# A fp32 decoder block on one core: reordered start, a shorter inverse root, and last stores from two queues

## The chip, the cores and the metric

The kernel runs on one core of one Trainium2 chip. The metric is device time in microseconds (us), the median of several runs. The profile is one execution of its own.

## The reference

The reference computes one decoder block on x of shape (1, 256, 2048) in float32:

```
x = x + 0.5 * swiglu(rms_norm(x, g1), wg1, wu1, wd1)     # 2048 -> 5632 -> 2048
h = rms_norm(x, gm)
b, c, xv, q, k, v = split(h @ w_in)                       # six parts of 1024 columns
y_conv = b * causal_depthwise_conv(c * xv, conv_w)        # 3 taps
a = softmax(q1 k1) - lam * softmax(q2 k2), causal         # 8 differential heads
y_attn = rms_norm(a @ v, subln_w) * (1 - lambda_init)
x = x + concat(y_conv, y_attn) @ w_out
x = x + 0.5 * swiglu(rms_norm(x, g2), wg2, wu2, wd2)
out = rms_norm(x, final_norm)
swiglu(x, wg, wu, wd) = (silu(x @ wg) * (x @ wu)) @ wd
```

## The kernel before

Every large product is a stream of weight chunks. A chunk is a [128, 2, 512] tile of float32 (512 KB: two blocks of 128 rows by 512 columns of a weight matrix). There are 656 of them, and each passes a ring of four slots (`RING = 4`) on its way: SyncE (SP) loads it into `raw[slot]` (`load`, L236 to L241), ScalarE (ACT) makes its high part `w_hi = fp32r(raw)` (`high`, L484 to L489), VectorE (DVE) makes its low part `w_lo = raw - w_hi` (`low`, L656 to L660), and TensorE (PE) multiplies (`unit`, L285 to L302). The activations are split in the same way into `xT_hi` and `xT_lo`. For each of two row tiles and two blocks of the chunk TensorE does three matmuls (hi by hi, hi by lo, lo by hi), so a chunk is 12 matmuls of 128x512.

Each engine runs a list of instructions written out by hand, in program order, and the engines meet at counting semaphores. The order around the change is therefore just the order of the statements:

- **Start.** SP loads a quarter of x (512 KB) and a chunk in turns, four times (L251 to L253), then goes on with chunks; a chunk from the fifth on waits for `lo_ready` of the one that had its slot. ACT first issues the loads of the column constants (`cols`, L571) and of the lambda rows (L572). TensorE turns the first two quarters of x (`turn_x`, L326 to L333, eight 128x128 transposes each, written to PSUM), does the first chunk, turns the third quarter, does the second chunk, turns the last quarter. ACT does `high(g)` and then `split_x` of quarter g, for g = 0 to 3 (L576 to L578); DVE does `low(g)` and the same split (L787 to L789). POOL (GpSimd) makes the identity matrix (L897 to L900) and then loads the final norm's weights, 1 MB when spread over 128 rows (`gfin`, L919). TensorE waits for chunk k's part of xT by `turned_lo`.
- **Inverse root.** `inverse_root` (L689 to L697) computes 1/sqrt of a mean of squares on VectorE: the mean (L691), a first guess from the bits in two steps (L692, L693), and three Newton steps of three instructions each (L695 to L697). Each one waits for the one in front of it (`link`, L98 to L101). It is used at the end of each of the first three norms' sums (`norm_factor`, both row tiles at once), once per head in the mixer (L828, eight heads), and for each row tile at the very end (`finish`, L712 to L723).
- **Mixer.** Two passes `j`, each of 48 chunks; the four heads' attention steps are laid between the chunks by their number `s`. The last step of a head: `inverse_root`, then `head = bank * orstd` (L830), then a transpose on TensorE (`turn_head`, L426 to L431). At a pass's end VectorE does the convolution (L866 to L874), ACT splits it (L638), and then both go back to the chunks.
- **End.** In the last pair of columns the last four chunks are done for row tile 0 first and then for row tile 1. For each tile VectorE adds the residual (L763), ACT squares it (L519), POOL multiplies by `gfin` (L932), `finish(t)` makes the factor, ACT scales the even groups of 512 columns (`scale_last`, L511), VectorE the odd ones (L723), and SP stores the four pieces of 256 KB in the order 0, 1, 2, 3 (L275 to L279).

Of the kernel before, what the change touches and what calls it, by code (L numbers as in the profile page):

```python
# [27 lines left out]
F32 = mybir.dt.float32  # L28
# [5 lines left out]
P = 128  # L34
# [25 lines left out]
MAGIC = float(0x5F3759DF)  # L60
NEWTON = 3

# [29 lines left out]
class Steps:  # L92
# [9 lines left out]

    def enter(self, i, each):

        self.outer, self.each, self.base, self.n = self.base + self.n, each, self.base + self.n + i * each, 0
# [6 lines left out]
def hybrid_block(nc, x_in, wg1, wu1, wd1, w_in, w_out, wg2, wu2, wd2, gf, columns, lambdas, out):  # L112
    ctx = ExitStack()
    with ctx:
# [16 lines left out]
        spare = sb("spare", [P, 1])  # L131
        ident = sb("ident", [P, P])
# [53 lines left out]
        gfin_loaded = sem("gfin_loaded")  # L186
        hi_ready = sem("hi_ready")
# [47 lines left out]
        def _(sp):  # L235
# [11 lines left out]
            def gate_up(base, wg, wu, c, first=False):  # L247
                for u, w in enumerate((wg, wu)):
                    for k in range(CD):
                        n = base + 2 * CD * c + CD * u + k  # L250
                        if first and u == 0 and k < XG:  # L251
                            load_x(k)
                        load(n, k % RING, w, k, c * W)  # L253
# [8 lines left out]
            gate_up(CH_FFN1, wg1, wu1, 0, first=True)  # L262
# [12 lines left out]
            for t in range(TT):  # L275
                for g in range(XG):
# [7 lines left out]
        def _(pe):  # L284
# [18 lines left out]

            def banks_free(pair, second):
# [21 lines left out]
            def turn_x(g):  # L326
                if g == 0:
                    pe.wait_ge(ident_ready, 2)
# [3 lines left out]
                for t in range(TT):  # L332
                    turn(x[:, :, g * W:(g + 1) * W], T_LOW if g % 2 == 0 else T_HIGH, t, turned)  # L333

            def gate_up(ch, pr, tbx, c, first=False, start=False):
                for second in range(2):
                    banks_free(pr + c, second)
                    for k in range(CD):
                        if first and second == 0:
                            pe.wait_ge(turned_lo, tbx + k + 1)  # L340
                        unit(ch + 2 * CD * c + CD * second, second, xT_hi, xT_lo, CD, k)
                        if start and second == 0 and k + 2 < XG:
                            turn_x(k + 2)
# [89 lines left out]

            turn_x(0)
            turn_x(1)
# [47 lines left out]
        def _(act):  # L483
# [7 lines left out]
            def split_x(tb, banks, gain, hi, k0):  # L491
                for b in range(2):
# [11 lines left out]

            def scale_last(t):
# [27 lines left out]
            def gate_up(ch, pr, hid, norm, c, first=False, start=False):  # L533
                base = ch + 2 * CD * c
                for n in range(2 * CD):
# [11 lines left out]
                    high(base + n + RING, n % RING)  # L547
                    if start and 2 <= n < 2 + XG:
# [22 lines left out]
            act.dma_start(cols[:], columns).then_inc(cols_loaded, 16)  # L571
            act.dma_start(lam_rows, lambdas.rearrange("(o a) d -> o a d", o=1).broadcast_to([P, 4, DK]))\  # L572
               .then_inc(lam_loaded, 16)

            act.wait_ge(cols_loaded, 16)
# [403 lines left out]
```

## Time and profile before

| | us |
|---|---|
| median of 3 runs | 1863.37 |
| lowest, highest | 1862.76, 1864.0 |
| span of the profiled execution, first to last instruction | 1861.2 |
| TensorE busy in it | 1835.5 |
| VectorE busy | 1128.0 |
| ScalarE busy | 834.9 |

The page gives the profiled execution's own time only as its span, 1861.2 us. The median of the runs is 2.2 us above that: what lies in front of the first and behind the last instruction, and what one execution differs from another. In the page the PE line is matmuls, PEld the weight loads beside them; a busy time is the union of instructions that overlap in the pipeline. Lines such as L295 are those of the kernel before.

### The profile page before, as it was taken

To read this page: it belongs to the slowest core of one execution; us is meant where nothing else is said; L and a number is where in the kernel's file an instruction comes from. 1 tells how busy PE (TensorE), PEld (TensorE's weight loads), DVE (VectorE), ACT (ScalarE), POOL (GpSimd) and SP (SyncE) were. 2 spreads that over 40 slices of the span, in tenths; PEclk is the share of its full clock that TensorE was granted. 3 is DMA by queue.
4 is the path that set the end of the run, shared out by engine and by line. 5 is a ranking of instruction groups with operands and counts; after the bars stand their busy time and mean duration, and the time that the engine had idled before them with its cause. 6 is when DMAs were issued, how large, how long until landed. Compare 5 with 4: busy or idle time off the path is not lost.

```text
span 1861.2 us, 24044 instructions
## 1 busy us (share of the span) xinstructions
PE 1835.5 (99%) x8184; PEld 1509.5 (81%) x8184; DVE 1128.0 (61%) x1519; ACT 834.9 (45%) x993; POOL 26.8 (1%) x36
## 2 busy tenths in 40 slices
PE   7999999999999999999999999999999999999997
PEld 6888888888888888888788788888888888888886
DVE  5666666666654554557547755666666666654554
ACT  6444444444444444455445444444444444443443
POOL 0000000000000000000000000000000000000000
PEclk9999999999999999999999999999999999999999
DMA  7666666666655556555564556666666666656653
GB/s 254 198 193 193 192 192 192 193 192 191 192 195 188 184 188 192 182 170 169 171 185 141 191 178 183 193 192 193 192 192 195 193 190 192 191 195 195 192 191 127
DMA packets 181155, 350.02 MB, mean 188 GB/s; under 512 B 10864, under 2 KB 10992, under 8 KB 180976
## 3 DMA queue, kind: packets, MB, share of 16 engines
q1 hardware_dynamic: 180672, 348.17, 61.0%
q0 software_dynamic: 144, 1.05, 0.1%
q8 instruction: 26, 0.43, 0.1%
q10 hardware_dynamic: 288, 0.17, 0.1%
q14 instruction: 25, 0.20, 0.0%
HBM read 347.25 MB, written 2.10 MB: 188 GB/s over the span
## 4 chain that ended last, share of the span: by engine, by line
PE 96%; DVE 1%; issue 1%; ACT 1%; DMA 1%; ACTq 0%; SPq 0%; DVEq 0%
PE bank L295 32%; PE bank L296 31%; PE bank L297 31%; PE bank L314 1%; DMA x<-in_x_dram 1%; PE bank L405 0%; ACT w_hi L489 0%; PE bank L422 0%; DVE turn_in L763 0%; PE bank L391 0%; DVE conv L871 0%; PE bank L413 0%; PE bank L430 0%; DVE nt L695 0%; DVE w_lo L659 0%
## 5 line engine op out<-in xcount | busy, mean ns | idle before, releaser
L659 DVE TENSOR_TENSOR w_lo<-raw,w_hi 128x1024 fp32r<-128x1024 f32 x656 | 808.7, 1235 | 694.3 <-ACT w_hi L489 692.4
L489 ACT ACTIVATE w_hi<-raw 128x1024 fp32r<-128x1024 f32 x656 | 693.3, 1059 | 875.8 <-PE bank L297 863.6
L295 PE MATMUL bank<-w_hi,xT_hi 128*128 128x512 f32 x1792 | 702.4, 392 | 1.6 <-DVE w_lo L659 1.5
L297 PE MATMUL bank<-w_hi,xT_lo 128*128 128x512 f32 x1792 | 698.4, 390 | 0.0
L296 PE MATMUL bank<-w_lo,xT_hi 128*128 128x512 f32 x1792 | 698.0, 390 | 0.0
L295 PEld LDWEIGHTS bank<-w_hi,xT_hi 128*128 128x128 f32 x1792 | 336.9, 188 | 73.8 <-issue 3.2
L297 PEld LDWEIGHTS bank<-w_hi,xT_lo 128*128 128x128 f32 x1792 | 336.8, 188 | 70.4
L296 PEld LDWEIGHTS bank<-w_lo,xT_hi 128*128 128x128 f32 x1792 | 337.1, 188 | 69.1
L295 PE MATMUL bank<-w_hi,hT_hi 128*128 128x512 f32 x704 | 276.7, 393 | 0.1
L296 PE MATMUL bank<-w_lo,hT_hi 128*128 128x512 f32 x704 | 275.8, 392 | 0.0
L297 PE MATMUL bank<-w_hi,hT_lo 128*128 128x512 f32 x704 | 274.2, 389 | 0.0
L679 DVE STREAM_TRANSPOSE gate<-turn_in 32x256 f32<-32x256 f32 x352 | 153.4, 436 | 5.7
L297 PEld LDWEIGHTS bank<-w_hi,hT_lo 128*128 128x128 f32 x704 | 132.1, 188 | 30.1
L295 PEld LDWEIGHTS bank<-w_hi,hT_hi 128*128 128x128 f32 x704 | 132.2, 188 | 29.4 <-issue 0.3
L296 PEld LDWEIGHTS bank<-w_lo,hT_hi 128*128 128x128 f32 x704 | 132.3, 188 | 27.3
L295 PE MATMUL bank<-w_hi,yT_hi 128*128 128x512 f32 x128 | 50.4, 393 | 0.0
L297 PE MATMUL bank<-w_hi,yT_lo 128*128 128x512 f32 x128 | 50.2, 392 | 0.0
L296 PE MATMUL bank<-w_lo,yT_hi 128*128 128x512 f32 x128 | 50.2, 392 | 0.0
L545 ACT ACTIVATE gate<-bank,rstd 128x512 f32<-128x512 f32 x44 | 30.1, 690 | 19.4 <-DVE hT_lo L686 10.5
L503 ACT ACTIVATE hT_hi<-gate 128x1024 f32 (+1 forms) x22 | 23.4, 1064 | 30.2 <-DVE gate L679 30.2
L740 DVE SCALAR_TENSOR_TENSOR turn_in<-bank,rstd,gate 128x512 f32<-128x512 f32 x44 | 30.9, 743 | 0.0
L295 PEld LDWEIGHTS bank<-w_hi,yT_hi 128*128 128x128 f32 x128 | 24.0, 188 | 5.6 <-issue 0.5
(95 smaller groups left out, 420.7 us busy)
## 6 DMA issues: line engine op xcount, KB each, us to landing
raw<-in_ffn_w_gate_dram SPq DMA_DIRECT2D x176, 512.0 KB, 3.8
raw<-in_ffn_w_up_dram SPq DMA_DIRECT2D x176, 512.0 KB, 3.7
raw<-in_ffn_w_down_dram SPq DMA_DIRECT2D x176, 512.0 KB, 3.8
raw<-in_w_in_dram SPq DMA_DIRECT2D x96, 512.0 KB, 3.7
raw<-in_w_out_dram SPq DMA_DIRECT2D x32, 512.0 KB, 3.8
x<-in_x_dram SPq DMA_DIRECT2D x4, 512.0 KB, 10.3
out_dram<-x SPq DMA_DIRECT2D x8, 256.0 KB, 3.2
gfin<-in_final_norm_dram POOLq DMA_DIRECT2D x1, 1024.0 KB, 9.6
```

Of the source, the lines that this page charges most:

```text
L295: pe.matmul(acc, hi[:, kt, ts], w_hi[slot][:, kk], start=(k == 0 and kk == 0), stop=False)
L296: pe.matmul(acc, hi[:, kt, ts], w_lo[slot][:, kk], start=False, stop=False)
L297: mm = pe.matmul(acc, lo[:, kt, ts], w_hi[slot][:, kk], start=False, stop=(k == chunks - 1 and kk == KC - 1))
L314: mm = pe.transpose(bank[banks[b]][:, kk * SEQ + t * P:kk * SEQ + (t + 1) * P], src[:, t, blk * P:(blk + 1) * P], ident[:])
L489: act.activation(w_hi[slot][:], raw[slot][:], ACT.Copy).then_inc(hi_ready, 1)
L503: act.activation(hT_hi[:, bass.ds(BT * c, BT), :], hidT, ACT.Copy).then_inc(hid_hi, 1)
L545: act.activation(gate[:, t], bank[t][:], ACT.Silu, scale=rstd[:, t:t + 1])\
L659: dve.tensor_tensor(w_lo[slot][:], raw[slot][:], w_hi[slot][:].bitcast(F32), ALU.subtract)\
L679: v = dve.transpose(dst[32 * j:32 * j + 32, :, :, i], src[32 * i:32 * i + 32, :, :, j])
L740: dve.scalar_tensor_tensor(out=turn_in[:, t], in0=bank[2 + t][:], scalar=rstd[:, t:t + 1], in1=gate[:, t], op0=ALU.mult, op1=ALU.mult).the ...
```

## The change

It has seven parts.

1. **Loads at the start** (SP). The first chunk comes in two halves of 256 KB (`first_chunk`), and the order is: quarter 0 of x, the two halves, chunk 1, quarter 1, chunks 2 and 3, quarters 2 and 3, then the other chunks. The lambda rows are loaded after ACT's fourth `high`, and `gfin` (POOL queue) after the first feed-forward's last save, some 740 us later.
2. **ScalarE at the start.** A one-element Silu in front of everything (`spare_out`), which loads the activation table; the later table load in front of the first real Silu is gone from the list. Then: half of the split of quarter 0, the first chunk's two halves, the other half of the split, chunk 1, the split of quarter 1, chunks 2 and 3. Quarters 2 and 3 are split between later chunks. VectorE follows the same order, and its small lambda work comes after the first norm factor.
3. **TensorE at the start.** 14 transposes of the identity into bank 7, which nobody reads, then quarter 0; then the first chunk in an order of its own (`first_unit`: hi by hi of both row tiles, lo of x by hi, hi by lo), quarter 1, chunk 1, quarter 2, chunks 2 and 3, quarter 3.
4. **Inverse root.** The guess is one instruction, each Newton step two, on `[P,1]` operands with one or two operands read as per-partition scalars. The results grow by a factor of 2^13, which is taken out by one more instruction in `norm_factor`, by a second multiplication in the head's scaling, and by `gfin` at the end. Where both row tiles are wanted (three norms, eight heads), each step is two instructions, one per tile, and each waits for the one before the last (`settle`).
5. **gfin scaled.** ACT multiplies `gfin` (128x2048) by 2^-13 behind the mixer's last pass.
6. **finish.** The sums of the first groups are divided by D and get EPS beforehand, so the mean is one instruction from `sq` and `ssum`.
7. **Last stores.** SP stores groups 1, 0, 3; ACT stores group 2 itself.

```diff
-MAGIC = float(0x5F3759DF)
+MAGIC = float(0x5F3759DF - 2 ** 31)
+GROWN = [3.0, 12.0, 768.0]
+SHRINK = 2.0 ** -13
+WARM = 14
...
@@ SyncE
+            def first_chunk(w):
+                src = w[0].rearrange("(k p) n -> p k n", p=P)
+                sp.dma_start(raw[0][:, 0], src[:, 0, 0:W]).then_inc(half_loaded, 16)
+                sp.dma_start(raw[0][:, 1], src[:, 1, 0:W]).then_inc(raw_loaded[0], 16)
...
-            gate_up(CH_FFN1, wg1, wu1, 0, first=True)
+            load_x(0)
+            first_chunk(wg1)
+            load(1, 1, wg1, 1, 0)
+            load_x(1)
+            load(2, 2, wg1, 2, 0)
+            load(3, 3, wg1, 3, 0)
+            load_x(2)
+            load_x(3)
+            gate_up(CH_FFN1, wg1, wu1, 0, opened=RING)
...
-                for g in range(XG):
+                for g in (1, 0, 3):
                     sp.wait_ge(scaled[g % 2], (t * XG + g) // 2 + 1)
@@ TensorE
+            def first_unit():
+                for kk in range(KC):
+                    pe.wait_ge(half_hi if kk == 0 else hi_ready, 1)
+                    if kk == 0:
+                        pe.wait_ge(turned_hi, TB_X1 + 1)
+                    for t in range(TT):
+                        pe.matmul(bank[t][:], xT_hi[:, kk, t * P:(t + 1) * P], w_hi[0][:, kk], start=(kk == 0), stop=False)
+                    if kk == 0:
+                        pe.wait_ge(turned_lo, TB_X1 + 1)
+                    for t in range(TT):
+                        pe.matmul(bank[t][:], xT_lo[:, kk, t * P:(t + 1) * P], w_hi[0][:, kk], start=False, stop=False)
+                    pe.wait_ge(half_lo if kk == 0 else lo_ready, 1)
+                    for t in range(TT):
+                        mm = pe.matmul(bank[t][:], xT_hi[:, kk, t * P:(t + 1) * P], w_lo[0][:, kk], start=False, stop=False)
+                mm.then_inc(chunk_used, 1)
...
+            pe.wait_ge(ident_ready, 2)
+            for _ in range(WARM):
+                pe.transpose(bank[7][:, 0:P], ident[:], ident[:])
             turn_x(0)
-            turn_x(1)
@@ ScalarE
+                act.wait_ge(scaled[0], (t + 1) * XG // 2)
+                act.dma_start(out[0, t * P:(t + 1) * P, cs], x[:, t, cs]).then_inc(stored, 16)
...
+            act.wait_ge(spare_ready, 1)
+            act.activation(spare_out[:], spare[:], ACT.Silu)
...
+            act.wait_ge(gfin_loaded, 16)
+            act.activation(gfin[:], gfin[:], ACT.Copy, scale=SHRINK).then_inc(gfin_scaled, 1)
@@ VectorE
-            def inverse_root(v_out, sums, y, width, t=slice(0, TT)):
-                link(dve.tensor_scalar(v_out, sums, 1.0 / width, EPS, ALU.mult, ALU.add))
-                link(dve.tensor_scalar(y.bitcast(I32), v_out.bitcast(I32), 1, None, ALU.logical_shift_right))
-                link(dve.tensor_scalar(y.bitcast(I32), y.bitcast(I32), -1.0, MAGIC, ALU.mult, ALU.add))
-                for _ in range(NEWTON):
-                    link(dve.tensor_tensor(nt[:, t], v_out, y, ALU.mult))
-                    link(dve.scalar_tensor_tensor(out=nt[:, t], in0=nt[:, t], scalar=-0.5, in1=y, op0=ALU.mult, op1=ALU.mult))
-                    link(dve.scalar_tensor_tensor(out=y, in0=nt[:, t], scalar=1.5, in1=y, op0=ALU.add, op1=ALU.mult))
+            def inverse_root(v, y, ts):
+                def each(make):
+                    for t in ts:
+                        steps.settle(len(ts) - 1)
+                        steps.mark(make(slice(t, t + 1)))
+                each(lambda t: dve.tensor_scalar(y[:, t].bitcast(I32), v[:, t].bitcast(I32), -0.5, MAGIC, ALU.mult, ALU.add))
+                for n in range(NEWTON):
+                    each(lambda t: dve.tensor_scalar(nt[:, t], y[:, t], y[:, t], v[:, t], ALU.mult, ALU.mult))
+                    each(lambda t: dve.tensor_scalar(y[:, t], nt[:, t], GROWN[n], y[:, t], ALU.subtract, ALU.mult))
+                steps.settle(0)
...
-                link(dve.tensor_tensor(ssum[:, ts], ssum[:, ts], sq[:, ts], ALU.add))
-                inverse_root(nv[:, ts], ssum[:, ts], rstd[:, ts], D, ts)
+                link(dve.tensor_scalar(nv[:, ts], sq[:, ts], 1.0 / D, ssum[:, ts], ALU.mult, ALU.add))
+                inverse_root(nv, rstd, (t,))
```

Three places show how the instructions stand. The first is ScalarE's list from its first row. Before:

```order
L571 DMA cols<-in_columns_dram 128x73
L572 DMA turn_in<-in_lambdas_dram 128x256
L489 ACT_TABLE_LOAD
L489 ACTIVATE w_hi0<-raw0 128x1024
L496 ACTIVATE xT_hi<-bank4,cols 128x256 x2
L496 ACTIVATE xT_hi<-bank5,cols 128x256 x2
L489 ACTIVATE w_hi1<-raw1 128x1024
L496 ACTIVATE xT_hi<-bank6,cols 128x256 x2
L496 ACTIVATE xT_hi<-bank7,cols 128x256 x2
L489 ACTIVATE w_hi2<-raw2 128x1024
L496 ACTIVATE xT_hi<-bank4,cols 128x256 x2
L496 ACTIVATE xT_hi<-bank5,cols 128x256 x2
```

and with the change:

```order
L644 DMA cols<-in_columns_dram 128x73
L646 ACT_TABLE_LOAD
L646 ACTIVATE spare_out<-spare 128x1
L554 ACTIVATE xT_hi<-bank4,cols 128x256 x2
L570 ACTIVATE w_hi0<-raw0 128x512
L572 ACTIVATE w_hi0<-raw0 128x512
L554 ACTIVATE xT_hi<-bank5,cols 128x256 x2
L547 ACTIVATE w_hi1<-raw1 128x1024
L554 ACTIVATE xT_hi<-bank6,cols 128x256 x2
L554 ACTIVATE xT_hi<-bank7,cols 128x256 x2
L547 ACTIVATE w_hi2<-raw2 128x1024
L547 ACTIVATE w_hi3<-raw3 128x1024
```

The table load and a one-element activation now stand ahead of all work, the lambda load (`turn_in<-in_lambdas_dram`) has moved back, the first chunk is two instructions of 512 columns, and the splits of quarter 0 (banks 4 and 5) stand around it.

The second is ScalarE at the end of the mixer's last pass, from the split of the convolution to the first chunks of the output projection. Before:

```order
L638 ACTIVATE yT_hi<-conv 128x1024
L590 REGISTER_ALU
L590 COMPARE_AND_BRANCH
L639 UNCONDITIONAL_BRANCH
L639 ISA
L488 REGISTER_ALU
L489 ACTIVATE w_hi<-raw 128x1024
L488 REGISTER_ALU
```

and with the change:

```order
L717 ACTIVATE yT_hi<-conv 128x1024
L669 REGISTER_ALU
L669 COMPARE_AND_BRANCH
L719 ACTIVATE gfin<-gfin 128x2048
L720 UNCONDITIONAL_BRANCH
L720 ISA
L546 REGISTER_ALU
L547 ACTIVATE w_hi<-raw 128x1024
L546 REGISTER_ALU
```

One activation over 128x2048 now stands between the last `yT_hi` and the next `w_hi`.

The third is VectorE behind the last residual (`turn_in<-bank,x`), the end of its list. Before:

```order
L763 SCALAR_TENSOR_TENSOR turn_in<-bank,x 128x512
L717 TENSOR_TENSOR ssum<-ssum,sq 128x1
L691 TENSOR_SCALAR nv<-ssum 128x1
L692 TENSOR_SCALAR rstd<-nv 128x1
L693 TENSOR_SCALAR rstd<-rstd 128x1
L695 TENSOR_TENSOR nt<-nv,rstd 128x1
L696 SCALAR_TENSOR_TENSOR nt<-nt,rstd 128x1
L697 SCALAR_TENSOR_TENSOR rstd<-nt,rstd 128x1
L695 TENSOR_TENSOR nt<-nv,rstd 128x1
L696 SCALAR_TENSOR_TENSOR nt<-nt,rstd 128x1
L697 SCALAR_TENSOR_TENSOR rstd<-nt,rstd 128x1
L695 TENSOR_TENSOR nt<-nv,rstd 128x1
```

and with the change:

```order
L865 SCALAR_TENSOR_TENSOR turn_in<-bank,x 128x512
L813 TENSOR_SCALAR nv<-sq,ssum 128x1
L788 TENSOR_SCALAR rstd<-nv 128x1
L790 TENSOR_SCALAR nt<-rstd,nv 128x1
L791 TENSOR_SCALAR rstd<-nt,rstd 128x1
L790 TENSOR_SCALAR nt<-rstd,nv 128x1
L791 TENSOR_SCALAR rstd<-nt,rstd 128x1
L790 TENSOR_SCALAR nt<-rstd,nv 128x1
L791 TENSOR_SCALAR rstd<-nt,rstd 128x1
L819 TENSOR_SCALAR x<-x,rstd 128x512 x2
```

Thirteen small instructions in a row have become eight, and the first of them reads `sq` as its tensor and `ssum` as a per-partition scalar.

## Rows read from the trace of the kernel before

**Rows 1.** The page: the chain that ended last, by engine

```profile
PE 96%; DVE 1%; issue 1%; ACT 1%; DMA 1%; ACTq 0%; SPq 0%; DVEq 0%
```

**Rows 2.** Waits of TensorE: engine, line, releaser: total us, times, longest us

```profile
PE bank L314 <- DMA x<-in_x_dram: 9.5, 2, 5.1
...
PE bank L295 <- DVE w_lo L659: 1.5, 1, 1.5
...
PE bank L430 <- DVE head L830: 1.0, 2, 0.5
```

**Rows 3.** Timeline from 5 to 28 us: start, us, engine, line, operation

```profile
5.08 1.94 PE L314 MATMUL bank<-ident,x 128*128 128x128 f32 x8 [5.08 <-DMA x<-in_x_dram]
...
8.07 1.28 ACT L489 ACT_TABLE_LOAD   x1 [8.07 <-DMA raw<-in_ffn_w_gate_dram]
9.37 1.06 ACT L489 ACTIVATE w_hi<-raw 128x1024 fp32r<-128x1024 f32 x1
10.33 1.55 ACT L496 ACTIVATE xT_hi<-bank,cols 128x256 fp32r<-128x256 f32 x4
...
11.40 1.97 PE L314 MATMUL bank<-ident,x 128*128 128x128 f32 x8 [4.38 <-DMA x<-in_x_dram]
...
17.44 0.44 PE L296 MATMUL bank<-w_lo,xT_hi 128*128 128x512 f32 x1
...
27.91 0.39 PE L295 MATMUL bank<-w_hi,xT_hi 128*128 128x512 f32 x1
```

**Rows 4.** Timeline, behind the last matmul

```profile
1851.46 0.63 ACT L519 ACTIVATE gate<-turn_in 128x512 f32<-128x512 f32 x1 [0.23 <-DVE turn_in L763]
1851.51 1.27 POOL L932 TENSOR_TENSOR x<-turn_in,gfin 128x512 f32<-128x512 f32 x1 [4.10 <-DVE turn_in L763]
...
1852.29 0.50 DVE L717 TENSOR_TENSOR ssum<-ssum,sq 128x1 f32<-128x1 f32 x1 [0.86 <-ACT gate L519]
1852.82 0.15 DVE L691 TENSOR_SCALAR nv<-ssum 128x1 f32<-128x1 f32 x1
...
1855.25 1.33 ACT L511 ACTIVATE x<-x,rstd 128x512 f32<-128x512 f32 x2 [3.07 <-DVEq L719]
1855.26 0.88 DVE L723 TENSOR_SCALAR x<-x,rstd 128x512 f32<-128x512 f32 x2 [0.16 <-DVE rstd L697]
```

**Rows 5.** Stretches of 1 us at the start; last number is GB/s

```profile
5.00:6.00 1.00, 0.92 (x5) 0.95 (x6) 0.00 (x0) 0.00 (x0) 0.00 (x0) 1.00 1.02 212
6.00:7.00 1.00, 1.00 (x5) 0.62 (x3) 0.00 (x0) 0.00 (x0) 0.00 (x0) 1.00 0.94 317
...
12.00:13.00 1.00, 1.00 (x7) 1.00 (x6) 1.00 (x4) 0.00 (x0) 0.00 (x0) 1.00 1.06 391
```

**Rows 6.** DMA issues of the page: KB each, us to landing

```profile
gfin<-in_final_norm_dram POOLq DMA_DIRECT2D x1, 1024.0 KB, 9.6
```

**Rows 7.** ScalarE by form: busy us, mean ns

```profile
L519 ACT ACTIVATE gate<-turn_in 128x512 f32<-128x512 f32 x24 | 14.8, 618 | 5.5 <-DVE turn_in L763 5.5
```

**Rows 8.** Timeline, last head of the second mixer pass

```profile
1028.37 0.16 DVE L691 TENSOR_SCALAR nv<-osq 128x2 f32<-128x2 f32 x1
...
1030.90 0.61 DVE L830 TENSOR_SCALAR head<-bank,orstd 128x128 f32<-128x128 f32 x2
...
1031.57 0.44 PE L430 MATMUL bank<-ident,head 128*128 128x128 f32 x2 [0.50 <-DVE head L830]
```

**Rows 9.** VectorE by form: busy us, mean ns

```profile
L853 DVE TENSOR_SCALAR rneg<-rinv,neg_lam 128x2 f32<-128x2 f32 x8 | 1.8, 229 | 0.3
```

**Rows 10.** Timeline, end of the mixer, ScalarE and VectorE

```profile
1044.84 2.94 ACT L489 ACTIVATE w_hi<-raw 128x1024 fp32r<-128x1024 f32 x3
...
1046.35 4.62 DVE L659 TENSOR_TENSOR w_lo<-raw,w_hi 128x1024 fp32r<-128x1024 f32 x4
```

**Rows 11.** Timeline of TensorE, output projection, fifth weight chunk

```profile
1047.94 0.39 PE L295 MATMUL bank<-w_hi,yT_hi 128*128 128x512 f32 x1
```

**Rows 12.** Timeline, last 11 us of the kernel

```profile
1850.64 7.15 SPq L279 DMA_DIRECT2D out_dram<-x  x8
```

More of the change, by code:

```diff
@@ L101, in link, with mark, settle @@
         self.eng.wait_ge(self.sem, self.base + self.n)
+    def mark(self, ins):
+        self.n += 1
+        ins.then_inc(self.sem, 1)
+    def settle(self, behind):
+        self.eng.wait_ge(self.sem, self.base + self.n - behind)
     def enter(self, i, each):
@@ L331, in turn_x @@
                 pe.wait_ge(x_loaded[g], 16)
-                for t in range(TT):
-                    turn(x[:, :, g * W:(g + 1) * W], T_LOW if g % 2 == 0 else T_HIGH, t, turned)
+                banks = T_LOW if g % 2 == 0 else T_HIGH
+                for blk in range(BT):
+                    for t in range(TT):
+                        mm = pe.transpose(bank[banks[blk // 2]][:, blk % 2 * SEQ + t * P:blk % 2 * SEQ + (t + 1) * P],
+                                          x[:, t, g * W + blk * P:g * W + (blk + 1) * P], ident[:])
+                    if blk % 2:
+                        mm.then_inc(turned, 1)
             def gate_up(ch, pr, tbx, c, first=False, start=False):
@@ L338, in gate_up @@
                     for k in range(CD):
+                        if start and second == 0 and k == 0:
+                            first_unit()
+                            turn_x(1)
+                            continue
                         if first and second == 0:
@@ L489, in high, with split_x @@
                 act.activation(w_hi[slot][:], raw[slot][:], ACT.Copy).then_inc(hi_ready, 1)
-            def split_x(tb, banks, gain, hi, k0):
-                for b in range(2):
+            def split_x(tb, banks, gain, hi, k0, halves=range(2)):
+                for b in halves:
                     act.wait_ge(turned, tb + b + 1)
@@ L547, in gate_up @@
                     high(base + n + RING, n % RING)
+                    if start and n in (1, 3):
+                        split_first(2 + n // 2)
                     if start and 2 <= n < 2 + XG:
@@ L660, in low, with split_first, first_low, split_x @@
                    .then_inc(lo_ready, 1)
-            def split_x(tb, banks, gain, hi, lo, k0):
-                for b in range(2):
+            def split_first(g):
+                split_x(TB_X1 + 2 * g, T_LOW if g % 2 == 0 else T_HIGH, cols[:, BT * g:BT * (g + 1)], xT_hi, xT_lo, BT * g)
+            def first_low():
+                dve.wait_ge(half_hi, 1)
+                dve.tensor_tensor(w_lo[0][:, 0], raw[0][:, 0], w_hi[0][:, 0].bitcast(F32), ALU.subtract).then_inc(half_lo, 1)
+                dve.wait_ge(hi_ready, 1)
+                dve.tensor_tensor(w_lo[0][:, 1], raw[0][:, 1], w_hi[0][:, 1].bitcast(F32), ALU.subtract).then_inc(lo_ready, 1)
+            def split_x(tb, banks, gain, hi, lo, k0, halves=range(2)):
+                for b in halves:
                     dve.wait_ge(turned_hi, tb + b + 1)
@@ L742, in gate_up @@
                     low(base + n + RING, n % RING)
+                    if start and n in (1, 3):
+                        split_first(2 + n // 2)
                     if start and 2 <= n < 2 + XG:
@@ L759, in residual @@
                             dve.wait_ge(squares_ready, q + g)
+                            if last and second == 1:
+                                dve.wait_ge(sums_taken, 4 * XG - 1)
+                                link(dve.tensor_scalar(ssum[:], ssum[:], 1.0 / D, EPS, ALU.mult, ALU.add))
                             dve.wait_ge(x_saved, r + g + 1)
```

82 lines of the change are left out of this document (53 added, 29 removed).

## The prediction

> **What bounds the kernel now.** I read the page first. TensorE is busy for 1835.5 of the span's 1861.2 us (the table above), and the chain that ended last is 96% PE [rows 1]. So the stream of chunks runs at TensorE's pace, and only time in which TensorE waits, runs at its lower clock, or is done already can be won. Next I read its waits [rows 2]: 9.5 us for two loads of x, 1.5 us once for a low part, 1.0 us in two waits for the scaled head. Then the timeline at both ends. At the start [rows 3] quarter 0 of x is turned at 5.08 us; the first chunk is there at 8.07, when ScalarE first loads a table for 1.28 us; quarter 1 comes at 11.40, and only then does steady work begin. Matmuls are 0.43 us apart up to 17.44 us and 0.23 us from there: TensorE's lower level (1.2 GHz) and its upper one (2.4 GHz). It rose 6.0 us after work became continuous at 11.40; the 1.94 us of transposes at 5.08 had not raised it. The fifth chunk starts at 27.91. At the end the last square begins at 1851.46 [rows 4], so some 10 us of the span are left to square, root, scaling and stores, with no matmul beside them.
>
> **Part 1, the start.** I time the changed start up to the same fifth chunk, since all later work there is alike.
>
> Loads. Quarter 0 keeps its place, so 5.08 us stands. Behind it the queue moved 212 KB in the sixth microsecond, 317 in the seventh, and 391 per us when it had the engines to itself [rows 5]. The halves (262 KB each) then have their last byte at about 6.2 and 7.0. The whole chunk landed 1.1 us behind its last byte (8.07 against 7.0); I take 0.8: 7.0 and 7.8. The 1 MB of `gfin`, 9.6 us under way among these loads [rows 6], and the lambda rows are gone, so each further 524 KB costs 1.34 us: chunk 1 at 9.1, quarter 1 at 10.4, chunks 2 and 3 at 11.8 and 13.1, quarters 2 and 3 at 14.5 and 15.8.
>
> ScalarE and VectorE. The table load ends before 5 us. Four transposes at the lower clock take half of 1.94 us, so half of quarter 0 is turned at 6.2. Its split takes half of 1.55 us [rows 3] to 7.1. The first half chunk takes 0.62 us (the nearest row of 512 columns, [rows 7]): 7.7. So TensorE starts its first matmul at 7.8; VectorE's low halves follow in about 0.7 us each, the first at 8.4.
>
> TensorE. Its 14 idle transposes run at 1.94/8 each from 1.6 to 5.0 us, quarter 0 to 7.0, a gap to 7.8. If they count as work like any other, the clock rises 6 us after 1.6, near 7.7. Then the first chunk (12 matmuls, 2.73 us) ends at 10.6; quarter 1 (0.87 us of transposes) at 11.5; chunk 1 waits for its low part to 11.6 and ends at 14.3; quarter 2 waits for its load at 14.5 and ends at 15.4; chunks 2 and 3 end at 20.9, quarter 3 at 21.7, and the fifth chunk starts at 21.8. **Gain: 27.91 - 21.8 = 6.1; I take 6.0.** The path touches loads, ScalarE and TensorE in turn, each within 0.3 us, so none gives more alone and each can take away. Bounds: the clock stays low to 12 us, 4.6; to 14 us, 3.6; all loads 1 us later, 5.2; half a microsecond earlier, 6.5.
>
> What is late next there: quarters 2 and 3 are split between later chunks, and the squares and the norm factor follow. By the same count the low part of the eleventh chunk is ready at about 36.7 and wanted at 38.2. Of the table load in front of the first Silu nothing was on the path. Nothing more is added for either.
>
> **Part 2, the heads.** The root with its mean took 2.53 us (1028.37 to 1030.90) [rows 8], 13 spacings of some 0.195. Now it has one instruction for the mean, then seven steps of two. The nearest row to a step that reads its operands as per-partition scalars takes 229 ns [rows 9]. If the two of a pair overlap, as the two of 0.35 us that took 0.61 together do [rows 8], a pair lasts about 0.265, the root 0.2 + 0.2 + 6 x 0.265 = 2.0 us. That wins 0.5 where TensorE waited 0.5 for the head [rows 8], twice [rows 2]: I take **0.9**. Other heads are covered by the chunk being multiplied, with about 0.5 us to spare. Bounds: +1.0 and, with no overlap, the last rival below. The three norm factors are covered by up to four chunks of the ring.
>
> **Part 3, gfin.** The load is moved to where the queue is half idle and behind no wait of the chunk stream: nothing; without that cover it would cost its 2.7 us. Its scaling on ScalarE is new and stands in front of the chunks. 1024 columns take 1.06 us [rows 3], 512 take 0.62 [rows 7]; 2048 then take 1.06 + 0.86, about 1.9. Before, `w_hi` began at 1044.84, the fifth low part at 1046.35 (VectorE was still busy with the convolution) and, at some 1.2 of the 4.62 us for four, ended near 1047.6 [rows 10]; TensorE took it at 1047.94 [rows 11]. Now `w_hi` of it ends at 1044.84 + 1.8 + 1.06 = 1047.7 and `w_lo` at 1049.0. TensorE waits 1.1 us: a new stall. **Cost 1.1**, bounds 0.6 and 1.6.
>
> **Part 4, the end.** From the mean's instruction at 1852.29 to the scaling at 1855.25 it was 2.96 us [rows 4]. Of it the first took 0.50 and ended when POOL's instruction (1851.51 + 1.27) ended. The new one has one tensor operand instead of two. Between 0.23 (not held) and 0.50 (held) I take 0.3; then 0.2 for the guess, 6 x 0.265, and 0.15 to the scaling: 2.25. Gain 0.7, bounds 0.3 and 1.1.
>
> The Trainium skill (SBUF — State Buffer) says that VectorE and GpSimd lock one port pair against each other, for a VectorE instruction with two SBUF inputs or in a two-port mode. The held instruction of [rows 4] agrees; by that rule the new one is free unless it runs in such a mode.
>
> Stores. The first store waited for ScalarE's first half of 1.33 us; now it waits for VectorE's first half of 0.88, so it goes 0.2 earlier. Four stores of 256 KB at 391 KB/us take 2.7 us, more than the 1.8 in which SP issues four (7.15 us for eight with a pause, [rows 12]). So the second queue wins nothing in itself; bounds 0 and 0.5. I take **0.9 for the end** in all. In the first tile ScalarE's own store comes ahead of its square for the second; the earlier root pays for it.
>
> **Sum.** 6.0 + 0.9 - 1.1 + 0.9 = 6.7 us. The span goes from 1861.2 to 1854.5. The median stands 2.2 above the span; I keep that distance: 1863.4 - 6.7 = **1856.7 us**.
>
> **Rivals.**
>
> A. The clock rises late. For it: the burst at 5.08 did not raise it, the rise came only with matmuls [rows 3], and the idle transposes leave a gap before real work. Against: they are the same instruction as that work's first 2 us. Rise between 11 and 14 us: the start gives 3.6 to 5.0, the time is 1857.7 to 1859.1. The Trainium skill (TensorE: Matmul & The Clock Gate, Part 1) says that the point of the rise differs from run to run of one kernel; this trace has one run, so it can't show it.
>
> B. The loads bound the start. Quarter 2 now stands behind chunk 3, and TensorE is at it when it lands. Loads 1 to 2 us later give 5.2 to 4.2: 1857.5 to 1858.5. With A, or with a larger stall at gfin, the gain can fall under 3.7 us.
>
> C. Slower: the pairs of the root don't overlap. Place: eight heads. Each of 14 instructions then costs 0.265, or 0.33 if two scalar operands cost more: the root takes 3.9 to 4.8 us instead of 2.5. The last heads of both passes lose 1.4 to 2.3 each, the other six, with 0.5 to spare, 0.9 to 1.8: 8 to 15 us together, against 5.8 from the rest. The time is 1866 to 1873. It decides the sign from a pair of about 0.49 us on (a root of 3.6). Against it: the overlapped pair in [rows 8]. The Trainium skill (VectorE: DVE Perf Modes, The DRAIN you can't avoid) says that the next instruction starts only when the pipeline is empty and that one should cut the number of instructions; by it this rival would be right. The row, two instructions in less than the sum of both, speaks otherwise.
>
> D. The change doesn't do what it says: the idle transposes run, but every start path waits for loads as before. The new order of instructions speaks against it.
>
> **How the numbers follow.** Forecast 0.60; A 0.17; B 0.12; A and B together or D, gain under 3.7, 0.07; C 0.04. The range 1855.3 to 1859.6 takes in the forecast with its bounds, A and B. A measurement can tell about 0.2%, 3.7 us, from no change: faster means under 1859.6. That is forecast, A and B with a little of each lost, 0.90; same 0.07; slower 0.03.
>
> **What would show it.** Right: first matmul near 7.8, matmuls 0.23 apart from there, fifth chunk near 22; ScalarE's 128x2048 instruction near 1.9 us with a wait of about 1.1 us on TensorE behind it; no wait for the head; 2.3 us from mean to scaling at the end. Wrong: matmuls 0.43 apart beyond 9 us (A), waits for quarter 2 (B), a root of over 3 us in the heads (C), or no wait at gfin, which would put the time 1 us lower.

## The result, and the profile after: slower, and where it went

The changed kernel takes **1870.54 us** (median of 5 runs, 1869.83 to 1870.71) against 1863.04 (5 runs beside it): 1.0038 times as long, 95% interval [1.0026, 1.005]. I had forecast 1856.7, and 1859.6 as the upper end. The profiled execution took 1870.6 us with a span of 1868.3, so the distance of the two is 2.3 us, much as before (2.2).

The chain of the page looks as before [rows 1]:

```profile
PE 96%; DVE 1%; issue 1%; ACT 1%; DMA 0%; DVEq 0%; ACTq 0%
```

TensorE's waits, in the columns of [rows 2], have shrunk: the 9.5 us for x are 0.8, and the heads cost 0.3 each in place of 0.5, where I had forecast no wait for them.

```profile
PE bank L327 <- DVE w_lo L740: 2.2, 2, 1.5
...
PE bank L382 <- DMA x<-in_x_dram: 0.8, 1, 0.8
PE bank L343 <- ACT w_hi L570: 0.7, 1, 0.7
PE bank L486 <- DVE head L941: 0.6, 2, 0.3
```

The start in the timeline, to be held against [rows 3]:

```profile
1.54 3.25 PE L492 MATMUL bank<-ident 128*128 128x128 f32 x14 [1.54 <-POOL ident L1010]
5.61 1.97 PE L382 MATMUL bank<-ident,x 128*128 128x128 f32 x8 [0.82 <-DMA x<-in_x_dram]
8.24 1.22 PE L343 MATMUL bank<-w_hi,xT_hi 128*128 128x512 f32 x2 [0.66 <-ACT w_hi L570]
9.26 1.05 PE L347 MATMUL bank<-w_hi,xT_lo 128*128 128x512 f32 x2
...
13.52 1.45 PE L382 MATMUL bank<-ident,x 128*128 128x128 f32 x8
14.73 0.48 PE L327 MATMUL bank<-w_hi,xT_hi 128*128 128x512 f32 x1
...
24.85 0.48 PE L327 MATMUL bank<-w_hi,xT_hi 128*128 128x512 f32 x1
```

The first chunk runs with 0.43 us from matmul to matmul, the lower level (1.2 GHz), up to its end at 13.5 us: the sign that the prediction had named for rival A. The fifth chunk starts at 24.85, before at 27.91; the forecast was 21.8. The end, for [rows 4]:

```profile
1860.45 0.21 DVE L813 TENSOR_SCALAR nv<-sq,ssum 128x1 f32<-128x1 f32 x1 [0.79 <-ACT gate L590]
1860.77 0.15 DVE L788 TENSOR_SCALAR rstd<-nv 128x1 int32<-128x1 int32 x1
...
1862.75 1.33 ACT L580 ACTIVATE x<-x,rstd 128x512 f32<-128x512 f32 x2 [2.33 <-DVEq L815]
```

2.30 us from mean to scaling, before 2.96. So the visible stalls have shrunk, the start's by half of what was said, the others' by about what was said, and still the kernel is 7.5 us longer. The first sign of the cause is in the groups by form, 128x512 matmuls whose stationary operand is `hT_hi` (busy us, mean ns of one). Before:

```profile
L295 PE MATMUL bank<-w_hi,xT_hi 128*128 128x512 f32 x1792 | 702.4, 392 | 1.6 <-DVE w_lo L659 1.5
L295 PE MATMUL bank<-w_hi,hT_hi 128*128 128x512 f32 x704 | 276.7, 393 | 0.1
L296 PE MATMUL bank<-w_lo,hT_hi 128*128 128x512 f32 x704 | 275.8, 392 | 0.0
```

and with the change:

```profile
L327 PE MATMUL bank<-w_hi,xT_hi 128*128 128x512 f32 x1788 | 699.6, 391 | 1.5 <-DVE w_lo L740 1.5
L327 PE MATMUL bank<-w_hi,hT_hi 128*128 128x512 f32 x704 | 278.4, 395 | 0.1
L328 PE MATMUL bank<-w_lo,hT_hi 128*128 128x512 f32 x704 | 278.1, 395 | 0.0
```

With xT nothing has changed for the worse; with hT each matmul shows 2 to 3 ns more, at the same shape, beside the same loads, at a granted clock of 1.00. Stretches show it plainly (instructions of TensorE in the brackets). One of the second gate/up stage (stationary xT) and one of the second down stage (hT), before:

```profile
1200.00:1580.00 380.00, 380.00 (x1678) 1.00 0.65 193
1620.00:1840.00 220.00, 220.00 (x962) 1.00 0.58 187
```

after:

```profile
1200.00:1580.00 380.00, 380.00 (x1678) 1.00 0.66 193
1620.00:1840.00 220.00, 220.00 (x945) 1.00 0.59 188
```

### The profile page after: what moved, and what is told of

It reads as the page before. It is cut to its first block, busy times and chain, and to the rows that moved or that the text cites. A ratio compares the mean times of both kernels' runs of the same rounds, so it can differ in the third digit from the quotient of the medians.

```text
span 1868.3 us, 24131 instructions
## 1 busy us (share of the span) xinstructions
PE 1850.1 (99%) x8198; PEld 1511.2 (81%) x8198; DVE 1130.8 (61%) x1548; ACT 835.1 (45%) x995; POOL 25.6 (1%) x36
## 4 chain that ended last, share of the span: by engine, by line
PE 96%; DVE 1%; issue 1%; ACT 1%; DMA 0%; DVEq 0%; ACTq 0%
PE bank L327 31%; PE bank L329 31%; PE bank L328 31%; PE bank L363 1%; ACT w_hi L547 0%; PE bank L461 0%; PE bank L478 0%; DVE conv L982 0%; DMA x<-in_x_dram 0%; PE bank L382 0%; PE bank L447 0%; DVE turn_in L865 0%; DVE w_lo L740 0%; PE bank L469 0%; DVE conv L985 0%
## 5 line engine op out<-in xcount | busy, mean ns | idle before, releaser
L329 PE MATMUL bank<-w_hi,hT_lo 128*128 128x512 f32 x704 | 278.1, 395 | 0.0
```

The lines of the kernel that those rows point to most:

```text
L329: mm = pe.matmul(acc, lo[:, kt, ts], w_hi[slot][:, kk], start=False, stop=(k == chunks - 1 and kk == KC - 1))
```

## Experiments

Two theories at first. **Placement**: the 32 bytes cost the 11 us, and the seven parts win what they show. **Code**: something in the changed instruction streams slows the down stages. The kernel before was run again beside each group of kernels: 1863.77 us beside the first four below, 1862.91, 1863.09 and 1862.97 beside the later groups. Ratios are to these.

### Is it the 32 bytes?

`slot_last`, the changed kernel with the tile allocated last:

```diff
-        spare_out = sb("spare_out", [P, 1])
         ident = sb("ident", [P, P])
...
+        spare_out = sb("spare_out", [P, 1])
```

> The changed kernel with its new one-element tile spare_out allocated behind all other tiles, so that hT and yT start where they did before (byte 134208, 64 above a multiple of 128; in the changed kernel 134240, 96 above). Placement theory: matmuls that take hT or yT are back at the spacing of before (229 ns in the second down projection, against 233.3 in the changed kernel), some 2500 of them at 4.4 ns win 11 us: about 1859.5 us, 0.998 of before. Rival (the matmuls are slowed by something else the change does, such as the late gfin load or the earlier schedule): spacing stays 233, time stays near 1870.5.

Measured 1859.2 us (8 runs), ratio 0.9972 [0.9962, 0.9983]. `before_pad32`, the kernel before with `pad = sb("pad", [P, 1])` behind `spare`:

> The kernel before with nothing but an unused one-element tile allocated behind spare; it moves hT and yT by 32 bytes to 134240, as the change does. Placement theory: spacing 233.3 ns in the second down projection, time 1863 + 11 = 1874 us (ratio 1.006). Rival: no difference, 1863.

Measured 1873.74, 1.0053 [1.0036, 1.007]. `after_pad32`, the changed kernel with one more such tile:

> The changed kernel with one more unused one-element tile, which puts hT and yT at 134272, a multiple of 128, where xT is too. Placement theory in its fuller form: spacing falls to the 226.7 ns that matmuls on xT show in both kernels, 6.6 ns less on 2112 matmuls and about as much on 384: about 1870.5 - 16 = 1854.5 us. Rival (only 32 against 64 counts, not 128): 229 ns, 1859.5 us. Rival (placement is nothing): 1870.5.

Measured 1852.49, 0.994 [0.9924, 0.9957], 2 us under what was expected; by the trace, its start is also 3.2 us ahead of the changed kernel's (fifth chunk at 21.60), which the change of placement doesn't explain (see the start, below). `before_pad64`, the kernel before with a pad of 64 bytes:

> The kernel before with an unused tile of nine elements (64 bytes): hT and yT at 134272, a multiple of 128. Placement theory in its fuller form: 2.3 ns less on some 2500 matmuls, about 1857.5 us. Rival (only 32 against 64 counts): 1863, no difference.

Measured 1857.6, 0.9968 [0.9955, 0.998]. So placement it is: the unused 4 bytes alone make the kernel before 10 us slower, 64 unused bytes make it 6.2 us faster, and both kernels have the same spacings at the same addresses. The second stretch of `after_pad32`, with 971 instructions where there were 962 and 945:

```profile
1620.00:1840.00 220.00, 219.91 (x971) 1.00 0.55 181
```

At equal placement the change wins: 4.6 us between the kernel before and `slot_last`, 5.1 between `before_pad64` and `after_pad32`.

### What of the address counts?

In all of these the start of hT was 0, 64 or 96 above a multiple of 128, and the least was the best. That would be a rule about the stationary tile alone. `moving32` puts the moving tiles off instead, by 32 bytes:

```diff
+        pad_a = sb("pad_a", [P, 1])
         w_hi = [sb(f"w_hi{i}", [P, KC, W], F32R) for i in range(RING)]
         w_lo = [sb(f"w_lo{i}", [P, KC, W], F32R) for i in range(RING)]
+        pad_b = sb("pad_b", [P, 17])
         x = sb("x", [P, TT, D])
```

> The kernel before with pads that put all the weight tiles that move through the array (w_hi, w_lo) 32 bytes above a multiple of 128, and xT, hT and yT on multiples of 128. If only the place of the stationary operand counts: the same time as the kernel before with a pad of 64 bytes, 1857.6 us, and the same 226.7 ns from matmul to matmul in all stages. If the place of any operand counts, or the distance of the two from each other: all stages are slower, by 2 to 6 ns for each of some 7900 matmuls, which is 1873 to 1905 us.

Measured **1915.29**, 1.028 [1.0264, 1.0296], with 234.3 ns in every stage, slower still than the 1873 to 1905 expected for the second case. The rule about the stationary tile alone falls. Its two stretches:

```profile
1200.00:1580.00 380.00, 380.00 (x1623) 1.00 0.65 186
1620.00:1840.00 220.00, 220.00 (x940) 1.00 0.60 187
```

`xT96_hT32` leaves the weights and moves the stationary tiles, by pads of 96 and 128 bytes:

```diff
+        pad_a = sb("pad_a", [P, 17])
         xT_hi = sb("xT_hi", [P, KD, SEQ], F32R)
...
         spare = sb("spare", [P, 1])
+        pad = sb("pad", [P, 25])
```

> The kernel before with pads that put xT (the stationary operand of both gate/up stages and the mixer) 96 bytes above a multiple of 128 and hT and yT 32 above one; the weight tiles stay on multiples of 128. If the place of the stationary tile is what costs, wherever it is read: gate/up now has 233.3 ns from matmul to matmul in place of 226.7, which over 5376 matmuls of the two gate/up stages and the mixer is 35 us, and down and out projection have a value of their own for 32 bytes, between 227 and 233 ns: 1892 to 1909 us. If only the distance from the end of the tiles or something of hT alone costs: gate/up stays at 226.7 and the time is 1858 to 1874 us.

Measured 1912.12, 1.0263 [1.0247, 1.0279]: 234.3 ns in gate/up (233.3 expected), 233.3 with hT, and so 3 us above the range. The cost goes to whichever stage reads the tile that stands off. `slots` gives each weight slot its own place:

```diff
-        w_hi = [sb(f"w_hi{i}", [P, KC, W], F32R) for i in range(RING)]
-        w_lo = [sb(f"w_lo{i}", [P, KC, W], F32R) for i in range(RING)]
+        w_hi, w_lo = [], []
+        for i in range(RING):
+            if i:
+                sb(f"pad_w{i}", [P, 1])
+            w_hi.append(sb(f"w_hi{i}", [P, KC, W], F32R))
+            w_lo.append(sb(f"w_lo{i}", [P, KC, W], F32R))
+        pad_b = sb("pad_b", [P, 1])
```

> The kernel before with the four slots of w_hi and w_lo at 0, 32, 64 and 96 bytes above a multiple of 128, and xT, hT and yT on multiples. If the place of the moving tile costs by itself: the chunks of slot 0 keep 226.7 ns from matmul to matmul, those of slot 1 have the 234.3 of the kernel with all slots at 32, slot 3 about the same, and slot 2 lies between; 1885 to 1902 us. If what cost there was that all the tiles behind the weights moved, and not the slot: the four slots do not differ.

Measured 1908.12, 1.0243 [1.0227, 1.0258], above the 1902 expected at most. Slots 0 to 3 have 233.3, 234.3, 233.3 and 233.0 ns. The slots do differ, against the second expectation, and **slot 0 did not keep 226.7**, against the first: its weights stand where they always stood, on a multiple of 128, and so does xT. What had changed is xT's place modulo 256, from 128 to 0. With that the values fall into line if one counts not the place of either tile but the distance of the stationary tile from the moving one modulo 256: 96 gave 234.3 in three kernels, from two pairs of places (modulo 256): moving 160 and stationary 0 in `moving32` and slot 1, moving 128 and stationary 224 in `xT96_hT32`. No run had moved both together, so three more were made. All go by the kernel with the 64-byte pad; `all128` and `all32` put 128 or 32 bytes ahead of `raw`, the first tile, and `far` puts 256 more ahead of xT and 256 more behind `spare`.

> The kernel before with a pad of 64 bytes behind spare, as in the run that took 1857.6 us, and 128 bytes ahead of all tiles, so that weights, xT, hT and yT all stand on a multiple of 256. Theory R (what counts is the distance of the stationary tile from the moving one, modulo 256): the distance is 0 everywhere, so 226.7 ns from matmul to matmul in all stages and 1857.6 us. Theory S (what counts is the stationary tile's own place, best 128 above a multiple of 256): all stages at 233 to 234 ns, 1908 to 1916 us.

> The same with 32 bytes ahead of all tiles in place of 128: weights, xT, hT and yT all 160 above a multiple of 256. Theory R: 226.7 ns and 1857.6 us. Theory S, or a rule that wants whole lines of 64 or 128 bytes for either tile: 228 to 235 ns in all stages, 1868 to 1920 us.

> The weights stay at 128 above a multiple of 2048, xT goes to 384 and hT and yT to 1664 above one, so that the distances from the weights are 256 and 1536, in place of 0 and 1024. If the distance counts modulo 256: 226.7 ns in all stages and 1857.6 us. If it counts modulo 512: gate/up and mixer at 233 to 235 ns, down and out projection at 226.7, 1893 to 1901 us. If modulo 1024: all stages slow, 1908 to 1920 us.

Measured 1857.38, 1857.12 and 1857.17 us, 226.7 ns in the gate/up and down stages of all three (the mixer, with other work between its chunks, has 227.6, as in every kernel at distance 0), as theory R said, with the modulus 256. `all32`, whose tiles all stand at an odd multiple of 32:

```profile
1200.00:1580.00 380.00, 380.00 (x1678) 1.00 0.66 192
1620.00:1840.00 220.00, 220.00 (x972) 1.00 0.58 184
```

All together, in ns from start to start, by stationary minus moving start, modulo 256:

| distance | ns | seen in |
|---|---|---|
| 0 | 226.7 | xT in both kernels; hT in the aligned ones; `all128`, `all32`, `far` |
| 32 | 233.0 | `slots`, slot 3 |
| 64 | 233.3 | `slots`, slot 2 |
| 96 | 234.3 | `moving32`; `slots`, slot 1; xT in `xT96_hT32` |
| 128 | 233.3 | `slots`, slot 0 |
| 160 | 233.3 | hT in `xT96_hT32` |
| 192 | 228.9 | hT in the kernel before and `slot_last` |
| 224 | 233.3 | hT in the changed kernel and `before_pad32` |

That it is the distance is shown at 0, with three pairs of places, and at 96, with two. Each of the other rows stands on one pair, so there the distance is the reading that fits all rows and not one tested by itself.

Why the distance counts is argued, not shown: the load of the next matmul's stationary operand lies beside the running matmul (PEld is busy 81% of the span), so both tiles are read at once. The Trainium skill (TensorE: Matmul & The Clock Gate, "Step-by-step: what each phase is for") gives TensorE two independent read ports for the two operands, and the Trainium skill (SBUF — State Buffer, "SBUF: two separate sides") says that TensorE never waits on anyone there. By these the two reads would not hold each other up. The measurement decides that the distance costs, up to 7.6 ns on 226.7; that the two reads are the reason no run shows.

### What is left of the start, the stall and the stores

At distance 0, three edits of `after_pad32`. `al_nowarm` has no idle transposes (`WARM = 0`):

> The changed kernel with 32 more bytes behind spare_out (which puts the tiles of hidden values and of y on a multiple of 128 bytes; 1852.5 us in its own run) and without the 14 idle transposes. If the idle transposes are what raises the clock early: TensorE's clock rises only behind 12 us in the trace, the fifth chunk starts at 24 to 25 us in place of 21.85, and the time is 1854.5 to 1855.5. If the early rise of that one profile was chance and the loads decide the start: no difference that can be measured, 1852 to 1853.

`al_fill` has 17, and 3 more behind quarter 0:

```diff
-WARM = 14
+WARM = 17
...
             turn_x(0)
+            for _ in range(3):
+                pe.transpose(bank[7][:, 0:P], ident[:], ident[:])
```

> The same aligned kernel with 17 idle transposes ahead of quarter 0 and 3 more behind it, so that TensorE stands still less before the first chunk. If the clock rises late in some executions because of that idle stretch: the clock is up before the first chunk, the fifth chunk starts at about 21.9, and the time is 1851.0 to 1852.0 with a smaller spread than the 1851.6 to 1853.4 of the aligned kernel. If the clock's rise does not follow from it: 1852 to 1853 as before, or up to 0.5 more, since three transposes more stand ahead of the first matmul.

Measured 1853.7 (1853.28 to 1854.62) and 1852.07 (1851.79 to 1852.5). So the 17 and 3 transposes are worth 1.6 us by the medians, less than the expectation for `al_nowarm` had it (1854.5 at least). In the traces it is 2.56: without them the first chunk ran 0.43 us apart and the fifth started at 24.71, with them at 22.15; the profiled execution of `al_nowarm` was its slowest. `al_fill` lies just above its 1851.0 to 1852.0, with the smaller spread that was expected. (The expectations count the fifth chunk 0.25 us later than rows of the timeline.)

What the 14 do varies, though in all four kernels that have them they ran 0.21 us apart, the lower level. In the changed kernel and in `slot_last` most or all of the first chunk was slow. In `after_pad32` quarter 0 was turned at the upper level, and the first chunk was fast from its first matmul on:

```profile
5.42 1.09 PE L383 MATMUL bank<-ident,x 128*128 128x128 f32 x8 [0.64 <-DMA x<-in_x_dram]
7.59 0.74 PE L344 MATMUL bank<-w_hi,xT_hi 128*128 128x512 f32 x2 [1.07 <-ACT w_hi L571]
...
21.60 0.50 PE L328 MATMUL bank<-w_hi,xT_hi 128*128 128x512 f32 x1
```

And in `al_gfin`, below, quarter 0 was turned at the upper level too and the first chunk was slow all the same, behind a gap of 1.07 us as in `after_pad32`:

```profile
1.54 3.10 PE L493 MATMUL bank<-ident 128*128 128x128 f32 x14 [1.54 <-POOL ident L1011]
5.70 1.10 PE L383 MATMUL bank<-ident,x 128*128 128x128 f32 x8 [1.06 <-DMA x<-in_x_dram]
7.87 1.22 PE L344 MATMUL bank<-w_hi,xT_hi 128*128 128x512 f32 x2 [1.07 <-ACT w_hi L571]
```

Windows of `al_gfin` (us, busy and count of TensorE, granted clock, DMA share, GB/s) show the fall in the clock's own column:

```profile
8.00:11.00 3.00, 3.00 (x7) 0.50 1.05 397
```

In `al_fill`, whose TensorE never stands for more than 0.39 us behind 1.54, the first chunk is fast:

```profile
1.54 3.89 PE L493 MATMUL bank<-ident 128*128 128x128 f32 x17 [1.54 <-POOL ident L1013]
5.53 1.91 PE L383 MATMUL bank<-ident,x 128*128 128x128 f32 x8
7.28 0.49 PE L496 MATMUL bank<-ident 128*128 128x128 f32 x3
8.16 0.73 PE L344 MATMUL bank<-w_hi,xT_hi 128*128 128x512 f32 x2 [0.39 <-ACT w_hi L573]
```

and was so in the two further profiles with the fill, below: three of three, against one of four with the 14. So few profiles point to the fill and don't prove it. Where the clock rises and falls behind the same instructions still differs from one execution to the next, and the cause of a single one stays open.

`al_gfin` moves the scaling behind the second feed-forward's first `gate_up` on ScalarE:

```diff
-            act.wait_ge(gfin_loaded, 16)
-            act.activation(gfin[:], gfin[:], ACT.Copy, scale=SHRINK).then_inc(gfin_scaled, 1)
             with act.Fori(0, XG // 2) as i:
                 residual(CH_OUT, PR_OUT, TB_X2, 2 * XG, XG, CD, False, i)
             gate_up(CH_FFN2, PR_FFN2, GROUPS, 3, 0, first=True)
+            act.wait_ge(gfin_loaded, 16)
+            act.activation(gfin[:], gfin[:], ACT.Copy, scale=SHRINK).then_inc(gfin_scaled, 1)
```

> The same aligned kernel with the scaling of gfin moved behind the last feed-forward's first column group, where ScalarE waits for TensorE anyhow. If the stall at 1050 us is this instruction's alone: the fall from the second pass to the output projection loses its 0.7 us idle and some slower matmuls, 1.2 us less, so 1851.0 to 1851.6. If ScalarE has no slack there either: the stall moves, and the time stays at 1852.5.

Measured 1850.56 (1850.36 to 1853.16), 1.5 us under `al_fill` beside it and below the 1851.0 to 1851.6 expected. The stall of the changed kernel was

```profile
1045.80 1.90 ACT L719 ACTIVATE gfin<-gfin 128x2048 f32<-128x2048 f32 x1
1047.60 3.89 ACT L547 ACTIVATE w_hi<-raw 128x1024 fp32r<-128x1024 f32 x4
1048.68 3.50 DVE L740 TENSOR_TENSOR w_lo<-raw,w_hi 128x1024 fp32r<-128x1024 f32 x3 [1.30 <-ACT w_hi L547]
1049.96 0.50 PE L327 MATMUL bank<-w_hi,yT_hi 128*128 128x512 f32 x1 [0.69 <-DVE w_lo L740]
```

and set matmul against matmul `al_gfin` gains 1.4 us just there on `after_pad32`. ScalarE at the new place waits some 1.66 us for TensorE between two `w_hi`, and TensorE shows no new wait there, so the 1.90 us fall into slack.

`best` has the fill and the moved scaling; `one_queue` is `best` with all last stores on SyncE:

```diff
-                for g in (1, 0, 3):
+                for g in (1, 0, 3, 2):
...
-                act.wait_ge(scaled[0], (t + 1) * XG // 2)
-                act.dma_start(out[0, t * P:(t + 1) * P, cs], x[:, t, cs]).then_inc(stored, 16)
```

> The changed kernel with 32 more bytes behind spare_out, 17 and 3 idle transposes, and gfin scaled behind the last feed-forward's first group: all that the runs so far point to. The sum of the parts: 1852.1 with the 17 and 3 transposes, less 1.5 of the moved scaling, 1850.6 us; range 1850.0 to 1851.2. If the two parts gain the same thing (a late clock in one execution and not another): 1850.6 to 1852.

> The same kernel with the last stores all on SyncE, in the order 1, 0, 3, 2. If the second queue wins nothing, as forecast: the same time within 0.2 us. If ScalarE's own store leaves earlier than SyncE's could: 0.2 to 0.6 us slower.

Measured 1850.82 (1850.5 to 1851.48; 1850.6 expected), 0.9935 [0.9921, 0.9948], and 1851.27 (1850.53 to 1852.46). `best` is 12.3 us faster than the kernel before and 19.7 faster than the changed one, and no faster than `al_gfin` by what 5 runs can tell. For the queues the medians differ by 0.45 us. By the number alone that is the expectation for a second queue that helps (0.2 to 0.6 slower without it), but it is less than the spread of either. In the traces the store gives next to nothing: from the start of the last matmul to the end of the span it is 9.8 us in `best` and 9.9 in `one_queue`.

## Why the prediction was wrong

The sign was wrong, and none of the rivals was the cause. The step that failed is in the first paragraph: "only time in which TensorE waits, runs at its lower clock, or is done already can be won". It takes for granted, and so does the **sum**, that the 7872 matmuls of 128x512 cost after the change what they cost before. Part 1, where the table load that `spare_out` is for is put at nothing ("Nothing more is added for either"), has no word of the tile itself. A term was missing: 2496 matmuls at +4.4 ns, +11.0 us. The trace of before held the sign of it, since hT matmuls stood at 393 and 392 ns beside 392 and 390 for xT (the groups by form); I took them for the same. I had read `spare_out` as a one-element activation and not as an allocation. With that tile put last, `slot_last` took 1859.2 us, inside the forecast's range of 1855.3 to 1859.6.

Term by term, by the matmuls of the two traces (predicted, in the changed kernel, then at equal placement between `before_pad64` and `after_pad32`):

| term | predicted | changed kernel | distance 0 |
|---|---|---|---|
| start | -6.0 | -2.96 | -5.91 |
| mixer, heads | -0.9 | -0.7 | -0.5 |
| gfin | +1.1 | +0.9 | +1.3 |
| end | -0.9 | -1.15 | -1.1 |
| distance of the tiles | none | +11.0 | 0 |
| sum | -6.7 | +7.1 | -6.2 |

The last column flatters the start: the trace of `after_pad32` is of its fastest execution (1851.58 us), and by the medians the change wins 5.1 us there, not 6.2.

- **Start.** The forecast of 7.8 for the first matmul and 21.8 for the fifth chunk met 8.24 and 24.85 in the changed kernel, 7.59 and 21.60 in `after_pad32`. Between the two lies rival A: the clock rises late in some executions, and I gave it 0.17; four of seven profiles with idle transposes had the first chunk fast throughout. In the changed kernel it rose only while quarter 1 was turned (the row at 13.52), and the start gave less than A's 3.6 to 5.0. The Trainium skill (TensorE: Matmul & The Clock Gate, Part 1), quoted there, says that the point of the rise differs from run to run; the four profiles behind the same 14 transposes agree. Of the loads (rival B) quarter 0 came 0.5 us later than forecast (turned at 5.61, not 5.08), a wait of 0.8; TensorE waited for none of the other quarters.
- **Heads.** The root fell from 2.53 to 2.35, not to 2.0. From pair to pair it is about 0.31 and not 0.265, since the instruction with two scalar operands takes 0.27 alone and a pair of it 0.45. So the two overlap, less than the row I took. Rival C (no overlap, 1866 to 1873 us) falls: the measured 1870.54 lies in its range by luck, from another cause. The Trainium skill (VectorE: DVE Perf Modes, "The DRAIN you can't avoid") has the next instruction wait for an empty pipeline, and adds that one that is not held starts earlier; two in 0.45 us, each 0.27 alone, agree with what it adds, and the prediction had quoted the first half alone.

```profile
1029.51 0.16 DVE L938 TENSOR_SCALAR nv<-osq 128x2 f32<-128x2 f32 x1
1029.71 0.21 DVE L788 TENSOR_SCALAR orstd<-nv 128x1 int32<-128x1 int32 x2
...
1029.90 0.46 DVE L790 TENSOR_SCALAR nt<-orstd,nv 128x1 f32<-128x1 f32 x2
1030.27 0.33 DVE L791 TENSOR_SCALAR orstd<-nt,orstd 128x1 f32<-128x1 f32 x2
...
1031.86 0.61 DVE L941 TENSOR_SCALAR head<-bank,orstd 128x128 f32<-128x128 f32 x2
```

- **gfin.** Right in place and size: 1.90 us on ScalarE, `w_hi` at 1047.60, then a wait of 0.69 on TensorE, with the granted clock at 1.00 behind it; set matmul against matmul the place costs 0.9.
- **End.** Right: 2.30 from mean to scaling for 2.25, and the mean was not held by POOL (0.21 in place of 0.50, though POOL's instruction ran from 1859.74 to 1861.01). The second queue gives nothing that 5 runs can show, as forecast.

## What to carry to other kernels

A change that adds a tile, even one of 4 bytes, moves the tiles behind it: list the start addresses of the matmul operands before and after, and keep the distance of the stationary tile from the moving one at a multiple of 256 bytes (seen here for fp32r matmuls of 128x512; no other was tried). When a sum of visible stalls comes out with the wrong sign, set matmul against matmul in the two traces, or count instructions in equal stretches where TensorE is always busy: a few ns on thousands of instructions shows in no wait. Idle matmuls ahead of the work can be worth having (1.6 us here, for 17 and 3), but what they bring is read from the spacing of the first real matmuls, and in more than one profile.

## What the hardware showed that I had not expected

- The distance table above: up to 3.4% of every 128x512 matmul, by where two tiles stand. At distance 0 the kernel before is 5.6 to 6.2 us faster with no other edit.
- The clock can go up and come back down within some microseconds: in `al_gfin` it was up at 5.70 (eight transposes in 1.10 us) and down at 7.87 (two matmuls in 1.22), behind 1.07 us of idle time. The same 1.07 us in `after_pad32` did not bring it down. In `al_gfin` the column of the granted clock shows 0.50. Ahead of the first rise it reads 1.00 though the engine is at the lower level: transposes 0.21 us apart in [rows 5] (0.11 at the upper level), matmuls 0.43 us apart in `al_nowarm` (its row below), so at the start the spacing of matmuls is what to read.

```profile
8.00:13.00 5.00, 4.73 (x11) 1.00 1.05 393
```

- Open: the mechanism behind the table, whether 128x512 is special in it, and why 192 is the mildest of the wrong distances.
